# Feed-forward input at the weights' place modulo 256 bytes, the first gather of a routed layer in two parts, and the token search read straight from PSUM

## The reference, cut to what matters

```
def ec_moe(h, w_router, w_gate, w_up, w_down):
    aff = jax.nn.softmax(logits, axis=-1)
    gates, idx = lax.top_k(aff.transpose(0, 2, 1), cap)        # cap = 32 of 256 tokens, 16 experts
    xs = h[idx]
    y = silu(xs @ w_gate) * (xs @ w_up) @ w_down               # 1024 -> 512 -> 1024
    y = y * gates                                              # added back at idx

h = h + 0.5 * _swiglu(_rmsnorm(h, norm_ffn1), wg, wu, wd)      # 1024 -> 2816 -> 1024, four times
```

## Time and profile before

| | us |
|---|---|
| median of 3 executions | 1672.04 |
| lowest, highest | 1664.42, 1673.15 |
| the profiled execution: its own time | 1669.61 |
| its span in the trace | 1667.5 |
| TensorE busy, its clock granted on average | 1438.0 (86%), 0.948 |
| VectorE busy | 922.9 (55%) |
| ScalarE busy | 684.2 (41%) |
| the four feed-forward networks | about 180 each |
| the two routed layers, from the search to the last scatter | about 211 and 215 |

### The profile page before, as it was taken

One profiled execution on the slowest core, in us unless ns is written; L12 is line 12 of the kernel. 1 busy time (PEld: TensorE's weight loads), 2 busy tenths in 40 slices (PEclk: granted clock), 3 DMA queues, 4 the chain that ended last, 5 costly groups with the idle time before them and its releaser, 6 DMA issues.

```text
span 1667.5 us, 24874 instructions
## 1 busy us (share of the span) xinstructions
PE 1438.0 (86%) x9548; PEld 1117.0 (67%) x9548; DVE 922.9 (55%) x1759; ACT 684.2 (41%) x1238; POOL 35.3 (2%) x48
## 2 busy tenths in 40 slices
PE   7987866678977656799999689999899998899998
PEld 6865432356654323588887468888788888778886
DVE  5674211157741111666667857666666668766666
ACT  5371110144711001544441445555555446664443
POOL 0000000001000000100000000000000000000000
PEclk9998987998989888899999989999999999999999
DMA  9818999995289999955554224455455453455510
GB/s 390 331 58 347 387 428 428 428 428 217 90 346 402 427 428 428 417 197 202 187 202 163 107 101 167 187 201 201 152 202 201 178 200 128 176 190 202 181 71 26
DMA packets 31614, 408.65 MB, mean 245 GB/s; under 512 B 3456, under 2 KB 5632, under 8 KB 7216
## 3 DMA queue, kind: packets, MB, share of 16 engines
q1 hardware_dynamic: 29088, 404.34, 61.1%
q10 hardware_dynamic: 2448, 3.24, 0.6%
HBM read 406.50 MB, written 1.06 MB: 244 GB/s over the span
## 4 chain that ended last, share of the span: by engine, by line
PE 70%; DMA 15%; DVE 9%; ACT 4%; issue 1%; POOL 1%; DVEq 0%; SPq 0%; POOLq 0%; ACTq 0%
PE bank L1813 20%; DMA ring<-stream 15%; PE bank L1817 10%; PE bank L1845 9%; PE bank L670 5%; PE bank L1851 4%; PE bank L1589 3%; PE bank L1607 3%; PE bank L676 2%; PE bank L611 2%; PE bank L1967 2%; PE bank L638 1%; PE bank L1520 1%; DVE near_both L461 1%; PE bank L2023 1%
## 5 line engine op out<-in xcount | busy, mean ns | idle before, releaser
L529 DVE TENSOR_TENSOR unit_lo<-ring,unit_hi 128x1024 fp32r<-128x1024 f32 x324 | 394.4, 1223 | 253.6 <-ACT unit_hi L524 253.2
L524 ACT ACTIVATE unit_hi<-ring 128x1024 fp32r<-128x1024 f32 x324 | 341.8, 1062 | 376.5 <-PE bank L1817 251.5
L1813 PE MATMUL bank<-near_both,unit_hi 128*128 128x512 f32 x1408 | 360.0, 396 | 3.0 <-DVE near_both L461 2.7
L1813 PEld LDWEIGHTS bank<-near_both,unit_hi 128*128 128x128 f32 x1408 | 256.7, 188 | 61.8 <-DVE near_both L461 4.8
L1817 PEld LDWEIGHTS bank<-near_both,unit_lo 128*128 128x128 f32 x1408 | 187.3, 188 | 16.1
L1817 PE MATMUL bank<-near_both,unit_lo 128*128 128x256 f32 x1408 | 189.7, 277 | 0.0
L1589 PE MATMUL bank<-ring,work 128*32 128x256 f32 x1792 | 121.7, 424 | 55.0 <-DMA ring<-stream 55.0
L1589 PEld LDWEIGHTS bank<-ring,work 128*32 128x32 f32 x1792 | 59.5, 119 | 112.9 <-DMA ring<-stream 71.8
L1845 PE MATMUL bank<-unit_hi,act_hi 128*128 128x512 f32 x336 | 131.3, 391 | 0.0
L1845 PE MATMUL bank<-unit_hi,act_lo 128*128 128x512 f32 x336 | 131.2, 390 | 0.0
L1751 DVE TENSOR_TENSOR work<-work,bank 128x128 f32<-128x128 f32 x32 | 9.2, 288 | 165.4 <-ACT work L1661 165.4
(11 more groups left out here) (312 smaller groups left out, 1909.3 us busy)
## 6 DMA issues: line engine op xcount, KB each, us to landing
ring<-stream SPq DMA_DIRECT2D x180, 2048.0 KB, 12.2
work<-ahead SPq DMA_DIRECT2D x4, 2048.0 KB, 10.1
ahead<-ahead SPq DMA_DIRECT2D x4, 2048.0 KB, 18.0
kept_slot<-ahead SPq DMA_DIRECT2D x2, 2048.0 KB, 23.9
ring<-stream SPq DMA_DIRECT2D x4, 512.0 KB, 7.5
work<-spread ACTq DMA_DIRECT2D x2, 1024.0 KB, 13.5
x<-x_in SPq DMA_DIRECT2D x2, 512.0 KB, 4.5
work<-final_rows ACTq DMA_DIRECT2D x2, 512.0 KB, 7.7
```

The costliest lines, as they stand in the source:

```text
L524: nc.scalar.activation(high_buf(name, u), raw_unit(name, u), ACT.Copy).then_inc(hi_done, 1)
L529: low = nc.vector.tensor_tensor(low_buf(name, u), raw_unit(name, u), high_buf(name, u).bitcast(F32), ALU.subtract)
L1813: nc.tensor.matmul(out[:, :], high[:, k, :], near_both[:, :, KD - 1 - k, :], start=(k == 0), stop=False, skip_group_check=True)
```

## The change

The feed-forward input gets a view `wide_both` that begins at `hT` itself, with its blocks in natural order; the four feed-forward networks write and read this one. "n8" keeps `near_both`. The first gather of each routed layer runs blocks 0 to 3, then half 0 of the first expert, then blocks 4 to 7. The fill of `ones` goes ahead of VectorE's wait, and the first round of the search reads the PSUM bank instead of a copy. The later gathers, in the loop, keep all eight blocks together.

```diff
+        wide_both = nc.alloc_sbuf_tensor_at("wide_both", [P, 2, KD, T], F32R, offset=hT_base)
+        wide_hi, wide_lo = wide_both[:, 0, :, :], wide_both[:, 1, :, :]
...
-        NEAR_TURNS = ("n4", "n6", "n7", "n8", "n9")
+        WIDE_TURNS = ("n4", "n6", "n7", "n9")
...
-                if name in NEAR_TURNS:
+                if name in WIDE_TURNS:
+                    high, low = wide_hi[:, k, :], wide_lo[:, k, :]
+                elif name == "n8":
                     high, low = near(near_hi, k), near(near_lo, k)
...
-        def gather_pe(pe, chosen_at):
-            for k in range(KD):
+        def gather_pe(pe, chosen_at, ks=range(KD)):
+            for k in ks:
...
             pe.wait_ge(route_dve, d + 4)
-            gather_pe(pe, lambda t: pick_g[:, t, :])
+            gather_pe(pe, lambda t: pick_g[:, t, :], range(4))
...
                         if half == 0:
                             spent(mm, na)
+                            if first and e == 0:
+                                gather_pe(pe, lambda t: pick_g[:, t, :], range(4, KD))
...
+            nc.vector.memset(ones, 1.0)
             v.wait_ge(route_pe, s + 2)
-            nc.vector.memset(ones, 1.0)
-            step(v, nc.vector.tensor_copy(scan_a, rank_bank[l][0][0:E, 0:T]))
-            src, dst = scan_a, scan_b
+            src, dst = rank_bank[l][0][0:E, 0:T], scan_b
             for _ in range(CAP // 8):
                 step(v, nc.vector.max(top8, src))
                 step(v, nc.vector.match_replace(dst, top8, src, -1.0))
-                src, dst = dst, src
+                src, dst = dst, (scan_a if dst is scan_b else scan_b)
...
-                    nc.tensor.matmul(out[:, :], high[:, k, :], near_both[:, :, KD - 1 - k, :], start=(k == 0), stop=False,
+                    nc.tensor.matmul(out[:, :], high[:, k, :], wide_both[:, :, k, :], start=(k == 0), stop=False,
                                      skip_group_check=True)
                 low_ready(pe, name, u, it)
                 for k in range(KD):
-                    mm = nc.tensor.matmul(out[:, 0:T], low[:, k, :], near(near_hi, k), start=False, stop=(k == KD - 1),
+                    mm = nc.tensor.matmul(out[:, 0:T], low[:, k, :], wide_hi[:, k, :], start=False, stop=(k == KD - 1),
                                           skip_group_check=True)
```

## The result

The changed kernel takes 1679.6 us (median of 7 runs, 1675.4 to 1686.9) where the kernel before takes 1670.8 beside it (7 runs, 1664.4 to 1673.7). The ratio is 1.0063 [1.0047, 1.0079], that is +10.5 us [7.9, 13.2]: slower, at the edge of the 0.5% that a measurement can tell from none, and inside the range of the prediction. The forecast had the sign right (+5.4 us) and about half of the size. The profiled execution took 1682.5 us with a span of 1680.4, 12.9 us above the one before.

A forecast was written before the change was run, and what follows sets the result against it. TensorE's matmul pace was taken to bound the feed-forward networks, the full DMA engines the routed loop. Input place +1.3 us and routed layers +4.1 us made +5.4 us on the median 1672.0: 1677 us, range 1662 to 1698.

The forecast's parts named there:

- Part 1: Feed-forward input's new place, 1408 matmuls at each of L1813 and L1817: -8.7 + 10.0 = +1.3 us.
- the step on the narrow matmul: L1817, 256 columns: pace rises from 0.113 to 0.120 us, taken from L676; +10.0 us over 1408 matmuls.
- The step on the wide one: L1813, 512 columns: pace falls from 0.233 to 0.227 us, taken from L1851; -8.7 us over 1408 matmuls.
- A: Both feed-forward matmuls pay, L1813 at 0.240 and L1817 at 0.120 us: +24 us, 1696 us; chance 0.22.
- B: Only the narrow feed-forward matmul pays, L1813 stays at 0.233 us: +14 us, 1686 us; chance 0.15.
- D: Only the wide feed-forward matmul gains, paces 0.227 and 0.113 us: -4.6 us, 1667 us; chance 0.15.
- E: Both feed-forward matmuls gain, L1817 by 3 ns: -4 us more, down to 1659 us; chance 0.06.
- Rival C: The feed-forward input's place does nothing to the paces: +4 us, 1676 us; chance 0.12.
- Part 2: Search in each routed layer: no copy and earlier fill -0.59 us, two PSUM reads +0.14, net -0.45 us per layer.
- Part 3: First gather in two parts: half 1 and the second group's stream start 2.7 us later, second layer 2.3 us later.
- rival F: Second routed layer: clock rises later, half 0 and late blocks run at 1.2 GHz, 1.8+1.6 us more, 1680; chance 0.04.
- The reading of the bounds: TensorE's pace bounds feed-forward networks; the DMA bounds the routed loop, where only the stream's start counts.

The follow-up runs named there:

- the place alone: Kernel before with only the feed-forward input 64 bytes higher, blocks in natural order; gather and search as before: 1672.5 us, ratio 1.0025.
- the places: Kernel before with only the feed-forward input moved, 0, 64, 128 or 192 bytes above the weights' place: ratios 1.0025, 1.0022, 1.0031, 1.0014.
- the search alone: Kernel before with only the search reading PSUM and the fill of `ones` under the wait: 1666.0 us, ratio 0.9988.
- the split alone: Kernel before with only the first gather of each routed layer in two parts: 1675.7 us, ratio 1.0047.
- the last version: Kernel before with the search from PSUM and four thrown-away matmuls of 512 columns during the search: 1666.2 us, ratio 0.9981.
- the kernel with the weights moved: Kernel before, input unmoved, high units of feed-forward networks and second mixer's output projection 64 bytes lower, half-sum scratch moved: 1673.3 us, 1.0026.
- +0: Kernel before with only the input moved to the weights' place modulo 256 bytes: ratio 1.0025, with blocks in reversed order 1.0023.
- +64: Kernel before with only the input moved, to 64 bytes above the weights' place, blocks in natural order: ratio 1.0022.
- +192: Kernel before with only the input moved, to 192 bytes above the weights' place, the old place modulo 256 bytes, natural block order: ratio 1.0014.

## Why the prediction was half right

**Part 1, the step on the narrow matmul, held:** 0.119 us against 0.120 taken from L676 of another projection. 1408 x 0.0047 = +6.6 us (busy time +6.7 in the place alone) against +10.0, since the merged row gave 0.113 for a mean of 0.1144. **The step on the wide one was over-sized:** mean distance down by 0.0046 us and not 0.006, 1408 x 0.0046 = -6.5 us (busy time -6.0) against -8.7. The two errors nearly cancel, so the term came out by luck in size: the four networks took 1.4 us more, forecast +1.3. The step that failed outright is "It touches 1408 matmuls at L1813 and 1408 at L1817": L1850 got slower too, by 1.5 ns over its 672, +1.0 us. The place alone measured +4.2 us [1.7, 6.7] against the forecast's +1.3; what lies beyond the networks was not in the forecast, and its cause is open (the lower clock of the executions at this place, above, is the candidate). Rivals A, B, D and E fall by the paces: 0.229 is not 0.240, nor the 0.233 of before, and the narrow one did pay. Rival C, that the place does nothing, falls too: the places show up to 6 us of busy time less on one line and up to 7 more on the other, at unchanged counts. The Trainium skill (SBUF — State Buffer, "SBUF: two separate sides") has TensorE never wait on anyone on the engines' side. What the prediction drew from it, that the place changes nothing, is refuted by these paces. The sentence itself is about other engines, and no run here tests it.

**Part 2 held in size.** Forecast -0.45 us per layer, found -0.65 from the turned affinities to the gather: the two instructions that read PSUM take 0.42 and 0.40 us, as their kind does from SBUF (0.42, and 0.40 for the replace of the kernel before at 141.46), so the +0.14 taken for them was 0. But 0.35 of it came back as a longer gather in the search alone.

**Part 3 held in its mechanism and was under-sized.** That the earlier first half buys nothing, that half 1 is late, and that the lateness reaches the issue of the second group whole, is what the rows show: half 1 later by 3.05 us after the gather's start (forecast 2.7), the issue by 3.2. The second layer was given 2.3 and took 2.5 in the split alone and 4.3 in the change. The missing part there is rival F: TensorE stopped for 1.23 us, the clock was still 0.50 for 3 us and 0.65 over the next four, and half 0 took 3.64 us and not 1.93. In the split alone the same stop stood there and half 0 took 1.93 us, as in the first layer of both profiles. So the stop does not decide it by itself; rival F is seen once in four such hand-overs (+1.8 us), and how often it strikes is not known from one profile of each kernel. The split alone measured +7.8 us [4.7, 11.0] against the 5.0 of its own terms (2.7 + 2.3). Its profile has 5.7 in the late issues. It also has 3.0 before the first gather and 2.1 between the first issue and the second gather, in code that the split does not touch; but that execution took 1680.4 us, 4.7 more than the median.

The sum: +1.3 + 4.1 forecast, +4.2 and +7.8 - 2.0 = +5.8 measured by the parts alone, 10.0 of the 10.5 us. So two terms share the error: part 1's (+2.9 over its forecast, none of it in the feed-forward networks) and part 3's (+2.8 over its own 5.0, of which the late issues show 0.7); part 2 gave 1.1 back. The change's own executions ran at a clock of 0.941 on average, against 0.947 of the kernel before beside the experiments; the forecast had no term for that. The lower ends of their intervals, 1.7 and 4.7, lie by the forecasts, so neither miss is sure by itself; that of the whole is, since 7.9 lies above 5.4. The reading of the bounds stands for these delays: from the second group's gather to the last scatter the first layer took 159.8 us before and 160.9 in the change, so the DMA-bound loop hid nothing of a late issue. For an early one it did not hold: of 1.6 us gained nothing was left in the first layer of the last version.

## What to carry to other kernels

Splitting work so that its first half starts sooner pays only if the first half's successor is what the critical resource waits for; here the stream's restart waits for the last half, and two hand-overs of some 1.25 us were put in its way. Where an engine is idle in front of a latency chain, a little work that nobody reads, sized to end before the chain's next step, can bring back the full clock behind it (3.84 us for the gather instead of 5.4 to 6.0); what that was worth to the whole kernel here is not told from the search alone. A change in where operands lie must be read from the paces of all matmuls that run beside them, the ones it doesn't touch too, and the clock of each stretch must be read before busy times are compared: two low starts made +4.2 us out of 1.7.

## What the hardware showed that was not expected

- The pace of a 128x512 matmul moved between 0.229 and 0.233 us and that of a 128x256 one between 0.114 and 0.119 with the input's place modulo 256 bytes alone, and of the places tried the one that is best for the one is worst for the other.
- Moving one operand changed the pace of matmuls that don't read it: 131.3 to 131.6 us for 336 at L1850, 89.8 to 91.3 us for 336 at L1853 of the kernel with the weights moved.
- With the input at +0 or +64 the granted clock, averaged over 10 to 12 executions, was 0.942 to 0.944, where the kernel before had 0.947 and the one at +192 0.948. The cause is open.
- Two hand-overs of the same form in the same place (1.23 us idle, then half 0) were followed by 3.64 us at a clock of 0.50 to 0.65 in one profiled execution and by 1.93 us in another.
- VectorE's maximum and replace took 0.42 and 0.40 us with 16x256 from PSUM, no more than from SBUF.
